# Final layer norm: row statistics of every second tile on ScalarE, tiles in pairs, and twelve idle products on TensorE

## The reference, cut to what matters

```python
ALPHA = (2 * DEPTH) ** 0.25
def layer_norm(x, g, b):
    xf = x.astype(jnp.float32)
    mu = xf.mean(-1, keepdims=True)
    var = jnp.square(xf - mu).mean(-1, keepdims=True)
    y = (xf - mu) * lax.rsqrt(var + LN_EPS) * g.astype(jnp.float32) + b.astype(jnp.float32)
    return y.astype(x.dtype)
...
f = moe(h.reshape(-1, D_MODEL), w_router, b_router, w_gate, w_up, w_down).reshape(h.shape)
return layer_norm(ALPHA * h + f, ln2_g, ln2_b)
```

## Time and profile before

| | us |
|---|---|
| median of 3 runs | 1109.3 |
| lowest, highest | 1108.87, 1111.01 |
| the profiled execution: its own time | 1110.12 |
| the profiled execution: span from first to last instruction | 1108.0 |
| mean granted TensorE clock | 0.936 of full |

### The profile page before, as it was taken

One profiled execution on the slowest core, in us unless ns is written; L12 is line 12 of the kernel. 1 busy time (PEld: TensorE's weight loads), 2 busy tenths in 40 slices (PEclk: granted clock), 3 DMA queues, 4 the chain that ended last, 5 costly groups with the idle time before them and its releaser, 6 DMA issues. The chain is left out here.

```text
span 1108.0 us, 13798 instructions
## 1 busy us (share of the span) xinstructions
PE 954.6 (86%) x5102; PEld 612.6 (55%) x5102; DVE 459.3 (41%) x1290; ACT 306.0 (28%) x600; POOL 163.9 (15%) x197
## 2 busy tenths in 40 slices
PE   2799879985589999999989999998599999999491
PEld 1566554543345566656655445543388787878140
DVE  4868869507032443444561432655500100100076
ACT  3421121442022243333451333422222121111322
POOL 3310400000120020110102010042200000000274
PEclk9998879997899999999998999999699999999796
DMA  9410020000896130110254112137586797966382
GB/s 245 151 52 20 0 81 29 29 28 18 319 424 248 23 98 1 39 60 1 69 200 154 40 38 78 40 152 303 211 287 228 257 380 239 381 227 225 120 320 107
DMA packets 59470, 164.06 MB, mean 148 GB/s; under 512 B 17256, under 2 KB 24463, under 8 KB 53895
## 3 DMA queue, kind: packets, MB, share of 16 engines
q1 hardware_dynamic: 53255, 140.84, 36.2%
q0 software_dynamic: 6144, 22.29, 5.6%
HBM read 108.65 MB, written 54.52 MB: 147 GB/s over the span
## 5 line engine op out<-in xcount | busy, mean ns | idle before, releaser
L1387 PE MATMUL banks<-xT,arena 128*128 128x384 f32 (+1 forms) x384 | 126.9, 487 | 20.3 <-DMA arena<-in_w_in 15.7
L2054 PE MATMUL banks<-arena,mixT 128*128 128x512 f32 x288 | 132.4, 606 | 0.0
L1387 PEld LDWEIGHTS banks<-xT,arena 128*128 128x128 f32 x384 | 73.0, 194 | 72.9 <-DMA arena<-in_w_in 12.4
L2054 PEld LDWEIGHTS banks<-arena,mixT 128*128 128x128 f32 x288 | 53.4, 194 | 56.6 <-issue 56.6
L1506 ACT ACTIVATE arena<-arena,mx 128x128 f32<-128x128 f32 (+8 forms) x72 | 58.5, 813 | 66.9 <-DVE mx L1598 66.3
L2218 PEld LDWEIGHTS banks<-mixT,v_tok 128*128 128x128 f32 x512 | 71.9, 194 | 4.5 <-issue 4.5
L2218 PEld LDWEIGHTS banks<-mixT,arena 128*128 128x128 f32 x512 | 70.4, 190 | 6.8 <-issue 6.8
L2218 PE MATMUL banks<-mixT,v_tok 128*128 128x160 f32 x512 | 72.5, 303 | 0.8 <-ACT mixT L2422 0.8
L2218 PE MATMUL banks<-mixT,arena 128*128 128x160 f32 x512 | 71.7, 300 | 0.8 <-ACT mixT L2422 0.8
L386 PE MATMUL banks<-xT,v_tok 128*128 128x384 f32 x192 | 72.1, 538 | 0.0
L793 PE MATMUL banks<-mixT,xT 128*128 128x512 f32 x144 | 62.8, 594 | 0.5 <-ACT mixT L858 0.5
(11 more groups left out here) (389 smaller groups left out, 1347.2 us busy)
## 6 DMA issues: line engine op xcount, KB each, us to landing
arena<-in_w_down SPq DMA_DIRECT2D x16, 1024.0 KB, 7.5
x_slots<-xT SPq DMA_DIRECT2D x4, 2048.0 KB, 20.6
y_park<-xT SPq DMA_DIRECT2D x4, 2048.0 KB, 39.0
v_tok<-in_w_gate SPq DMA_DIRECT2D x8, 1024.0 KB, 5.3
v_tok<-in_w_up SPq DMA_DIRECT2D x8, 1024.0 KB
arena<-in_w_gate SPq DMA_DIRECT2D x8, 1024.0 KB, 5.5
arena<-in_w_up SPq DMA_DIRECT2D x8, 1024.0 KB
arena<-x_slots SPq DMA_DIRECT2D x16, 512.0 KB, 5.2
```

Of the source, the lines that this page charges most:

```text
L1387: last = T.matmul(b[:, 0:cn], w[:, k, :], xT[:, k, c0:c0 + cn], start=(k == 0), stop=(k == KD - 1))
L2054: last = T.matmul(bank[half], mixT[:, k, t * P:(t + 1) * P], w_oh[half][:, k, :], start=(k == 0), stop=(k == KD - 1))
```

## The change

Three things change, all in the final stage.

1. Ahead of TensorE's final loop twelve products are issued that nobody reads: `ident` times 512 columns of `h_all`, into the high halves of the four bank pairs. They wait for nothing but the engine's own order.
2. Tiles go in pairs (0,1), (2,3), (4,5), (6,7), and tile 8 alone. The even tile of a pair and tile 8 keep the statistics on VectorE. Those of the odd tile are taken on ScalarE: a Copy pass over the 128x1024 tile with row sums as an accumulator output, and, once VectorE has made the negated mean of it, a Square pass with that mean as bias, again with row sums. VectorE makes variance plus epsilon of that in one small operation. Both passes write their main output to `junk`, a free stretch of mixT.
3. The orders become, for a pair (t, t+1): VectorE: sum t, statistics t, gain t-1, sum t+1, reciprocal and bias t, negated mean t+1, gain t, variance t+1, reciprocal and bias t+1. ScalarE: root t, sum pass t+1, normalise t, square pass t+1, root t+1, normalise t+1.

TensorE:

```diff
                 overflow(pe, released, body, done)
 
+                for n in range(12):
+                    T.matmul(duo[n % 4][:, 512:1024], ident[:, :], h_all[:, 0, 0:512], start=True, stop=True)
                 for t in range(NT):
```

ScalarE:

```diff
-                for u in range(NT):
+                def sums(u):
+                    s = u % SLOTS
+                    rows = slice(0, min(P, TOK - u * P))
+                    act.wait_ge(s_sum, u + 1)
+                    S.activation(junk[u][rows, :], h_all[rows, u, :], ACT.Copy,
+                                 accum_out=st2[s][rows, 0:1]).then_inc(s_p1, 1)
+
+                def squares(u):
+                    s = u % SLOTS
+                    rows = slice(0, min(P, TOK - u * P))
+                    act.wait_ge(s_nm, u // 2 + 1)
+                    S.activation(junk[u - 1][rows, :], h_all[rows, u, :], ACT.Square, bias=st2[s][rows, 18:19],
+                                 accum_out=st2[s][rows, 13:14]).then_inc(s_sq, 1)
...
+                for u in range(0, NT, 2):
+                    deviation2(u)
+                    if u + 1 < NT:
+                        sums(u + 1)
+                    normal(u)
+                    if u + 1 < NT:
+                        squares(u + 1)
+                        deviation2(u + 1)
+                        normal(u + 1)
```

`deviation2` and `normal` hold the lines of L2486 to L2490 unchanged. VectorE:

```diff
-                for t in range(NT):
...
+                def negated_mean(t):
+                    s = t % SLOTS
+                    rows = slice(0, min(P, TOK - t * P))
+                    dve.wait_ge(s_p1, t // 2 + 1)
+                    V.tensor_scalar(st2[s][rows, 18:19], st2[s][rows, 0:1], -1.0 / D, None, ALU.mult).then_inc(s_nm, 1)
+
+                def variance(t):
+                    s = t % SLOTS
+                    rows = slice(0, min(P, TOK - t * P))
+                    dve.wait_ge(s_sq, t // 2 + 1)
+                    V.tensor_scalar(st2[s][rows, 14:15], st2[s][rows, 13:14], 1.0 / D, EPS, ALU.mult, ALU.add).then_inc(s_var2, 1)
...
+                for t in range(0, NT, 2):
+                    add(t)
+                    statistics(t)
                     if t:
                         gain(t - 1)
...
+                    if t + 1 < NT:
+                        add(t + 1)
+                    scale_shift2(t, 12, -1.0)
+                    if t + 1 < NT:
+                        negated_mean(t + 1)
+                    gain(t)
+                    if t + 1 < NT:
+                        variance(t + 1)
+                        scale_shift2(t + 1, 18, 1.0)
```

More of the change, by code:

```diff
@@ L1788, in hybrid_step @@
             dg = [[vflat[:, P * (2 * t + c):P * (2 * t + c + 1)] for c in range(2)] for t in range(NT)]
+            junk = [mall[:, D * t:D * (t + 1)] for t in range(NT)]
             st2 = [mem.enter_context(nc.sbuf_tensor(f"ln2_st{s}", [P, 20], F32)) for s in range(SLOTS)]
@@ L1885, in hybrid_step @@
             s_v2 = sem("f_vector_chain")
+            s_p1 = sem("f_row_sums")
+            s_nm = sem("f_negated_mean")
+            s_sq = sem("f_squares_summed")
             s_var2 = sem("f_variance")
@@ L2482, in _, with deviation2 @@
                         S.activation(dg[t][c], ident[:, :], ACT.Copy, scale=wsel[:, t, c:c + 1]).then_inc(s_dg, 1)
-                for u in range(NT):
+                def sums(u):
[10 more added lines that the diff above has]
+                                 accum_out=st2[s][rows, 13:14]).then_inc(s_sq, 1)
+                def deviation2(u):
                     s = u % SLOTS
@@ L2487, in _, with normal @@
                     S.activation(st2[s][rows, 15:16], st2[s][rows, 14:15], ACT.Sqrt).then_inc(s_std2, 1)
+                def normal(u):
+                    s = u % SLOTS
+                    rows = slice(0, min(P, TOK - u * P))
                     act.wait_ge(s_nb2, u + 1)
@@ L2871, in _, with add @@
                 dve.wait_ge(s_g2[0], 16)
-                for t in range(NT):
-                    s = t % SLOTS
+                def add(t):
                     rows = slice(0, min(P, TOK - t * P))
@@ L2877, in _, with statistics @@
                                            ALU.mult, ALU.add).then_inc(s_sum, 1)
+                def statistics(t):
+                    s = t % SLOTS
+                    rows = slice(0, min(P, TOK - t * P))
                     dve.wait_ge(s_sum, t + 1)
@@ L2882, in _, with scale_shift2 @@
                     V.tensor_scalar_add(st2[s][rows, 14:15], st2[s][rows, 13:14], EPS).then_inc(s_var2, 1)
+                def negated_mean(t):
[4 more added lines that the diff above has]
+                def variance(t):
+                    s = t % SLOTS
+                    rows = slice(0, min(P, TOK - t * P))
+                    dve.wait_ge(s_sq, t // 2 + 1)
+                    V.tensor_scalar(st2[s][rows, 14:15], st2[s][rows, 13:14], 1.0 / D, EPS, ALU.mult, ALU.add).then_inc(s_var2, 1)
+                def scale_shift2(t, col, sign):
+                    s = t % SLOTS
+                    rows = slice(0, min(P, TOK - t * P))
+                    dve.wait_ge(s_std2, t + 1)
+                    chain2(V.reciprocal(st2[s][rows, 16:17], st2[s][rows, 15:16]))
+                    V.tensor_scalar(st2[s][rows, 17:18], st2[s][rows, col:col + 1], st2[s][rows, 16:17], sign,
+                                    ALU.mult, ALU.mult).then_inc(s_nb2, 1)
+                for t in range(0, NT, 2):
+                    add(t)
+                    statistics(t)
                     if t:
                         gain(t - 1)
[L2885 to L2889, removed]
+                    if t + 1 < NT:
[7 more added lines that the diff above has]
+                        scale_shift2(t + 1, 18, 1.0)
 _INS = ["x_prompt", "x_sample", "cache_k", "cache_v", "cache_logf", "page_table", "state_ssm_re", "state_ssm_im",
```

## The result

| | before | after |
|---|---|---|
| median of 10 runs, us | 1109.41 | 1114.45 |
| lowest, highest | 1105.05, 1111.01 | 1111.28, 1117.16 |
| profiled execution: own time, span | 1110.12, 1108.0 | 1116.04, 1114.3 |

The ratio of after to before is 1.0049, with a 95% interval of 1.0034 to 1.0064: the kernel is slower by 5.4 us (3.8 to 7.1). That is the distance of the means; the medians of the table lie 5.0 apart. The forecast had been 6.5.

What follows compares the result with a forecast made beforehand. The end was taken as set by the first sum's start, the stretch to tile 8's sum, paced by VectorE, and an unchanged 14.8 us tail; head +3.2 and pairs +3.3 on 1109.3 gave 1115.8 us, range 1109.6 to 1119.0.

Steps and rivals of the forecast that it cites:

- The gap: TensorE's idle 13.4 us before the final tiles: a branch holds its sequencer 3.94 us, only 7.11 us are free.
- rival 1: At TensorE's overflow branch: stall gone or hardly there, first sum 2.8 us earlier, +0.5 in all, 1109.8; chance 0.12.
- The head's size: Start of the first sum: 24 idle passes of 0.43 us outlast the free 7.11, so it comes 3.2 us later.
- The pair: VectorE's work on two tiles: 9.6 us (9.5 to 9.9) against 2 x 4.34 = 8.68.
- The three waits: VectorE waiting for ScalarE in each pair: 0.9 us for row sums, 1.0 at the normalised tile, 0.4 in the root's round trip.
- Pairs together: All four pairs in the final tiles: +3.3 us (2.6 to 4.5), 0.6 from the first and 2.7 from the others.
- The sum: Head and pairs together: 3.2 + 3.3 = +6.5 us on the whole kernel.
- (2): In the pairs: ScalarE's passes hide and VectorE's saving stays, -5.8 with the head's +3.2, 1106.7; chance 0.06.
- (3): On ScalarE: Square is not in Sqrt's table, two loads of 1.28 us a pair, +10.2, 1126; chance 0.03.
- (4): In the pairs: VectorE's gains meet GpSimd's shifts, +0.7 x 4 to +2 x 4, up to 1124; chance 0.03.

Runs made afterwards that it cites:

- The short body: The changed kernel with TensorE's overflow body written out for one tile in place of nine; ratio 1.0014 against the kernel before.
- the pairs alone: The changed kernel without its twelve idle products; ratio 1.0015 against the kernel before.
- the products alone: The kernel before with the twelve idle products behind the overflow branch and nothing else; ratio 1.0013 against the kernel before.
- spread pairs: The kernel before with tiles 0 to 5 paired, VectorE's small operations that wait for ScalarE put one pair later, no idle products; ratio 1.0013.

## Why the prediction was right

**The gap.** I had read the idle 13.4 us in two parts, with the sequencer held for the first. It held: 4.22 us, products from 6.66 after the last expert product (I had 6.3). The short body shows the cause, and it also makes rival 1 real: with the branch at 0.37 the head is 1.4 ahead of the profile of before (the rival had 2.8, without the fall of the clock just after the products began). Rival 1 had its mechanism and its place right; it just doesn't happen with this body.

**The head's size.** I said +3.2, and the trace has +2.5: 24 passes of 0.43 and the 0.3 us that the branch took longer, less 1.0 because the half clock lasted 3.6 us and not 5.7. I had let that cost cancel; it varies from run to run, 3.1 to 5.7 us of products in the traces where it had fallen well before them. The 5.7 are those of the profile that I built on, the others are 3.1 to 3.7. Against the head of the pairs alone the products cost 3.65, my 3.2 and the longer branch. So the step was right where the clock is like, and that the trace has +2.5 and not 3.6 is chance.

**The pair.** 9.6 predicted, 9.46 measured. The Copy pass, which no row had, took 1.06 against my 1.05 from the two other rows; the read of its sums added 0.09 to it, as in the earlier trace rows. The three waits were foreseen as 0.9, 1.0 and 0.4 and came as 0.89, 0.98 and 0.27. Pairs together: +3.3 predicted; 37.16 - 34.58 = +2.6 measured. The difference is the steady pair (0.14 three times) and the first one, 8.8 in place of 9.1. The +2.6 too is measured against a stretch that holds the unexplained wait of 0.57; against the products alone, where it is missing, it is 3.25.

**The sum.** 6.5 against 5.1 in the traces and 5.4 (3.8 to 7.1) in the runs. Both terms were a little too large against that profile, the head by 0.7 and the pairs by 0.7. The runs' interval holds the 6.5, so they don't decide between it and 5.1.

**The rivals.** The passes don't hide (2): the waits stand in the rows. Square needs no table of its own (3). VectorE and GpSimd don't meet in the changed kernel (4): all its gains but the last take 1.22. (The shift that the last gain met in the kernel before is tile 7's, from 1097.25 to 1099.60; the one at 1100.76 in the earlier trace rows comes behind it.) But I had filed that rival as a detail of the change, and it is what holds back every attempt to do better: with an earlier first sum or spread pairs the meetings come, and cost 1.1 to 1.2 us each with the first and 0.6 to 1.3 with the second.

## What to carry to other kernels

Before filling an engine's idle time, ask what its sequencer does in it: a bracket that names a DMA tells what ended the wait, not what the first half was. Work that needs no input is best queued ahead of a long branch, where the array runs it while the sequencer is held. When work moves to an idle engine, count the handovers, not the instructions: here 1.44 us were saved on the busy engine in each pair and 2.2 us came back (2.14 of them as waits), because the next instruction in its order needed the other engine each time.

## What the runs showed of the hardware

- TensorE's branch over a body written out for nine tiles took 3.4 to 4.25 us in ten executions, and 0.37 us over a body for one tile. The other engines' branches over their shorter bodies took 0.05 to 0.08.
- A gain on VectorE (two inputs in SBUF, 1.22 us) beside a shift on GpSimd took 1.84 to 2.54 and ended about 1.1 us after the shift. The sum with one input in PSUM kept its 1.21 beside the same shifts. A gather issue on GpSimd that began while a gain ran grew too, from 0.94 to between 1.22 and 1.96, and ended about 0.8 us after the gain.
- TensorE's clock stayed full where the products stood ahead of the branch, with 0.92 us of idle time before them and 0.8 to 1.6 behind (four executions). Where they stood behind it, it fell each time: in the run with the short body (2.8 us idle) 0.5 us after they began, in the three with 6.4 to 6.7 us idle about 3 us before.
